# Inverse roots of all norms: from logarithm and exponential on ScalarE to a square root on ScalarE and a reciprocal on VectorE

## The chip, the cores and the metric

The kernel runs on one core of one Trainium2 chip, as one program. The metric is the device time of one execution in microseconds (us). Three runs of the kernel before took 2928.62, 2932.60 and 2936.35 us; their median, 2932.6 us, is the number to compare with.

## The reference, cut to what matters

Two blocks of two layers each work on 512 tokens of 1024 features (the second block has 256 context tokens beside them, so its first layer works on 768). Every layer is: norm, input projection, mixer, output projection, norm, gated feed-forward with a short convolution. What the change touches is the inverse root in all the norms:

```python
def rmsnorm(x, g):                       # first block; rmsnorm_2 of the second is the same
    xf = x.astype(jnp.float32)
    y = xf * lax.rsqrt(jnp.mean(xf * xf, axis=-1, keepdims=True) + EPS)
    return (y * g.astype(jnp.float32)).astype(x.dtype)

# token_mixer of the first block: each head's output is normed, gained and gated
ht = ht * lax.rsqrt(jnp.mean(ht * ht, axis=-1, keepdims=True) + EPS)
m_out = ht.reshape(B, S, MLSTM_W) * mh_norm_g * jax.nn.sigmoid(mo)

# retention_output of the second block: a group norm over each head's 64 values
mu = jnp.mean(y, axis=-1, keepdims=True)
var = jnp.mean((y - mu) ** 2, axis=-1, keepdims=True)
yn = ((y - mu) * lax.rsqrt(var + EPS)).reshape(B, L, RET_DIM) * gn_g
return silu(gate) * yn

# a layer of the first block
h = rmsnorm(x, g_pre_mix);  y = token_mixer(h, ...);  x = x + rmsnorm(y, g_post_mix)
h = rmsnorm(x, g_pre_ffn);  y = conv_ffn(h, ...);     x = x + rmsnorm(y, g_post_ffn)
```

## The kernel before

Features lie on the 128 partitions, tokens in the free dimension. A weight matrix comes as tiles of 128 output features; TensorE multiplies in float32r, and each product is made of three matmuls (high part by high part, high by low, low by high), `pe_chunk`, line 1011. So every weight tile and every activation is split in two: the high part by ScalarE (`split_high`, line 850, writes WH), the low part by VectorE (`split_low`, line 856, writes WL). Weight tiles go through a ring of 4 or 6 buffers.

A `Run` is a list of parts, each a head (the norm that makes the activations HH and HL of a part) and its segments (the projections). Each engine has its own program, written out in order: `scalar`, `vector`, `tensor`, `gpsimd` and `sync` of `Run`. The order of work on an engine is the order of that text; semaphores (`Signal`) tie the engines together.

The places with an inverse root:

- `Rstd` (lines 371 to 388) turns a mean of squares in PSUM bank pair PS[2] into RSTD, 128 partitions by 512 or 768 tokens. `act` does a logarithm (line 380) and an exponential with scale -0.5 (line 382) on ScalarE, and `wait` is what VectorE calls before it first reads RSTD. There are 13: four "late" ones in `GainHead` (512 tokens; the projection is computed from the unnormed rows and its result is multiplied by RSTD, line 970 into U or line 2211 into Z), four "first" ones (512 tokens; three in `GainHead`, one in `NormHead`: they scale Y, line 597, which is added to X, line 660 or 719), four in `NormHead` before line 727 (768 tokens in three, 512 in one), and one in `FinalHead` before line 767 (512), whose eight results are stored.
- `MixHead` (line 445): the same on MEAN2, 128x512, once in each layer of the first block. TensorE waits for it before the fourth chunk of the first three tiles (`begin`, line 484).
- `RetentionHead` (lines 507 to 588): three of 768 tokens in the first layer of the second block and three of 512 in the second. TensorE makes the three variances between the first and the second tile (line 579); ScalarE does the three logarithms (line 522), splits a weight tile, and does the three exponentials (line 527). VectorE splits that weight tile's low part (line 551), then does for each of the three rows a gain (line 555) and a gating (line 559), and then the low parts of activation chunks 5, 6 and 7 (line 537). TensorE goes through chunks 0 to 4 of tiles 1 and 2 meanwhile, and then needs chunk 5.

After the mean of squares TensorE does not stand still at once: `tensor` (line 1051) queues 24 small dummy matmuls (`idle`, line 257, 48 instructions) in which no result is used, and only then waits for the first chunk of HL (line 647 in `GainHead`, line 738 in `NormHead`). From that chunk on it takes three tiles chunk by chunk.

ScalarE evaluates its functions from a table set; `preload_act_table_set` loads a set ahead of its use, and where a function isn't in the loaded set a load stands right before it (an ACT_TABLE_LOAD with the function's line).

Of the kernel before, what the change touches and what calls it, by code (L numbers as in the profile page):

```python
# [10 lines left out]
ACT = mybir.ActivationFunctionType  # L11
AX = mybir.AxisListType

P = 128
D = 1024
# [98 lines left out]
def build(nc, a, out):  # L114
    ctx = ExitStack()
    with ctx:
# [129 lines left out]
        ysq_done, ysq_added = S("ysq_done"), S("ysq_added")  # L246
        log_done, rstd_done = S("log_done"), S("rstd_done")
        xsq_done, xsq_summed = S("xsq_done"), S("xsq_summed")
# [122 lines left out]
        class Rstd:  # L371
# [6 lines left out]
            def act(self, act):  # L378
                n = self.tokens
                act.activation(RSTD[:, 0:n], PS[2][:, 0:n], ACT.Ln, bias=EPSC[:, 0:1]).then_inc(log_done.sem, 1)  # L380
                act.wait_ge(log_done.sem, log_done.at(self.n + 1))
                act.activation(RSTD[:, 0:n], RSTD[:, 0:n], ACT.Exp, scale=-0.5).then_inc(rstd_done.sem, 1)  # L382

            def wait_log(self, eng):
                eng.wait_ge(log_done.sem, log_done.at(self.n + 1))

            def wait(self, eng):
                eng.wait_ge(rstd_done.sem, rstd_done.at(self.n + 1))

# [34 lines left out]
        class MixHead(Head):  # L424
# [20 lines left out]
            def act(self, act):  # L445
                act.activation(MEAN2, MEAN2, ACT.Ln, scale=float(D // P)).then_inc(head_ln.sem, 1)
                self.copied(act, 3)
                act.wait_ge(head_ln.sem, head_ln.at(1))
                act.activation(MEAN2, MEAN2, ACT.Exp, scale=-0.5).then_inc(head_rstd.sem, 1)
                for h in range(4):  # L450
                    act.wait_ge(head_out.sem, head_out.at(h + 1))
                    self.copied(act, 4 + h)
                for u in range(3, self.run.ring):
                    self.run.split_high(act, u)

            def dve(self, dve):
# [36 lines left out]
        class RetentionHead(Head):  # L493
# [13 lines left out]
            def act(self, act):  # L507
                n = self.tokens
                act.activation(Z[:, RG:RG + 3, 0:n], Z[:, RG:RG + 3, 0:n], ACT.Silu).then_inc(gate_done.sem, 1)  # L509
                act.preload_act_table_set("natural_log")  # L510
                self.copied(act, 0)
                self.copied(act, 1)
                self.run.split_high(act, 0)
                for c in range(3):
                    act.wait_ge(centred.sem, centred.at(c + 1))
                    act.activation(GROUP[c][:, 0:n], Z[:, RQ + c, 0:n], ACT.Square).then_inc(group_sq.sem, 1)
                for c in range(2, 5):
                    self.copied(act, c)
# [12 lines left out]
                for u in range(3, self.run.ring):  # L531
                    self.run.split_high(act, u)
# [7 lines left out]
            def dve(self, dve):  # L540
# [25 lines left out]
            def begin(self, pe, seg):  # L566
# [7 lines left out]
                for i, tile in enumerate(first):  # L574
                    if i == 1:
                        for c in range(3):
# [4 lines left out]
                            ins.then_inc(var_ps.sem, 1)  # L581
                        pe.wait_ge(group_ln.sem, group_ln.at(3))
                    for k in range(5):
# [8 lines left out]
        ROWS2 = [PO, PO + 1, NV, NV + 1, NV + 2, RG, RG + 1, RG + 2]  # L592
        mean_ps, centred, group_sq, var_ps, group_ln, group_rstd, group_out, gate_done = (
            S(n) for n in ("mean_ps", "centred", "group_sq", "var_ps", "group_ln", "group_rstd", "group_out", "gate_done"))

# [4 lines left out]
        class GainHead(Head):  # L600
# [72 lines left out]
        class NormHead(Head):  # L673
# [16 lines left out]
            def act(self, act):  # L690
                n = self.tokens
                self.before.wait_mean(act)
                if self.gain:
                    self.first.act(act)
                    act.preload_act_table_set("natural_log")
                    act.wait_ge(ctx_in.sem, ctx_in.at(16))
# [46 lines left out]
            def pe(self, pe):  # L743
                if self.gain:
                    self.first.wait_log(pe)
                    for c in range(DC):
# [29 lines left out]
        class Run:  # L776
# [149 lines left out]
            def act_out(self, act, tile):  # L926
# [25 lines left out]
                else:  # L952
                    if seg.squares and t == 0:
                        act.preload_act_table_set("natural_log")
                    if seg.out_act:
# [157 lines left out]
        def stream(run, mixer=None):  # L1113
# [35 lines left out]
            if parts[0][0].ready:  # L1149
                done(head_ln=1, head_rstd=1, head_ps=4, hg_done=4, head_out=4)  # L1150
            elif parts[0][0].begins:
                done(mean_ps=3, centred=3, group_sq=3, var_ps=3, group_ln=3, group_rstd=3, group_out=6, gate_done=1)
            done(**{f"w_loaded{s}": 16 * len(range(s, n, ring)) for s in range(ring)}, w_hi=n, w_lo=n, unit_done=n,
                 acc_free=tiles, own_done=run.n_hid, tap_done=run.n_hid, filtered=run.n_late,
                 silu_done=run.n_hid // 2, gated=run.n_hid // 2, g_hi=run.n_hid // 2, g_lo=run.n_hid // 2,
                 sq_done=run.n_sq, sq_added=run.n_added, sq_summed=run.n_summed,
                 ysq_done=run.n_ysq, ysq_added=run.n_ysum, log_done=run.n_rstd,
                 rstd_done=run.n_rstd, xsq_done=run.n_x, xsq_summed=run.n_x, t_done=run.n_t, h_hi=run.n_h,
# [3 lines left out]
        def region(offset, size):  # L1162
# [29 lines left out]
        qk_own, conv_done, qk_done = S("qk_own"), S("conv_done"), S("qk_done")  # L1192
        head_ln, head_rstd, head_ps, hg_done, head_out = (
            S(n) for n in ("head_ln", "head_rstd", "head_ps", "hg_done", "head_out"))
        ROWS1 = [AQ1, AQ1 + 1, AQ1 + 2, AQ1 + 3, V1, V1 + 1, V1 + 2, V1 + 3]
# [3 lines left out]
        class MixPrep:  # L1199
# [11 lines left out]
            def pe(self, pe, run, tile):  # L1211
                if tile.t == 7:
                    tile.seg.head.late.wait_log(pe)
                    pe.wait_ge(acc_free.sem, acc_free.at(tile.n - 6))
# [68 lines left out]
        def mix1(VEC, ahead):  # L1283
# [43 lines left out]
            with block() as b:  # L1327
# [131 lines left out]
                def _(act):  # L1459
# [45 lines left out]
                    for s in steps:  # L1505
# [21 lines left out]
                        if a + 1 == U - 1:  # L1527
                            act.preload_act_table_set("natural_log")

# [991 lines left out]
```

## Time and profile before

| | us |
|---|---|
| median of three runs | 2932.6 (2928.62 to 2936.35) |
| the profiled execution, its own time | 2934.65 |
| its span, first to last instruction | 2932.9 |
| TensorE busy in the span | 2856.3 (97%) |
| VectorE busy | 1763.2 (60%) |
| ScalarE busy | 1160.9 (40%) |
| GpSimd busy | 150.0 (5%) |

Every time below comes from the one profiled execution. L12 is line 12 of the kernel's text, PE is TensorE, DVE is VectorE, ACT is ScalarE. The granted TensorE clock was 0.995 of full speed over the span. In the timelines a row gives the start in us from the span's beginning, the duration of one instruction or of several that follow each other (x2 and so on), engine, line, operation, what it writes and reads, and in brackets how long the engine had stood idle before it and what ended that.

### The profile page before, as it was taken

Reading aid. Unit: us, or ns where it says so; the run is one execution under the profiler, and the core shown is the slowest. Engines: PE = TensorE matmul, PEld = TensorE weight load, DVE = VectorE, ACT = ScalarE, POOL = GpSimd, SP = SyncE. Lnnn points to the kernel's source line nnn. Section 1 sums busy time; section 2 is a strip of 40 time slices with the busy share of each in tenths; the row PEclk is TensorE's granted clock in tenths of the full one; section 3 lists DMA queues with packets and bytes.
Section 4 is the critical chain, followed back from the end, with each engine's and each line's share of the span. In section 5 each row is a group of like instructions: output and inputs, shape, how many; then the busy total and the mean of one; then the engine's idle time right before and its main releaser. Section 6 shows DMA issues by size and latency. Waiting matters only on the chain. (4 is left out here: it accounts for less than half of the span.)

```text
span 2932.9 us, 35827 instructions
## 1 busy us (share of the span) xinstructions
PE 2856.3 (97%) x14618; PEld 2408.2 (82%) x14618; DVE 1763.2 (60%) x2639; ACT 1160.9 (40%) x1709; POOL 150.0 (5%) x172
## 2 busy tenths in 40 slices
PE   9999999999999999999988999999999999999999
PEld 7657888878467888889965999999999975788887
DVE  6667866768567767667665565435534137564563
ACT  5255524443345424342255343213323236543342
POOL 0101000010110000000020100000000002100001
PEclk9999999999999999999999999999999999999999
DMA  5303243343112243326620111121122220232322
GB/s 204 108 15 108 93 134 105 93 130 122 44 59 86 90 147 100 116 85 232 212 66 30 58 58 65 57 73 65 58 58 65 65 97 23 101 101 84 111 83 83
DMA packets 84180, 269.95 MB, mean 92 GB/s; under 512 B 9264, under 2 KB 12208, under 8 KB 83632
## 3 DMA queue, kind: packets, MB, share of 16 engines
q1 hardware_dynamic: 84016, 267.66, 27.9%
q8 instruction: 116, 1.90, 0.3%
q14 instruction: 48, 0.39, 0.0%
HBM read 265.52 MB, written 2.10 MB: 91 GB/s over the span
## 5 line engine op out<-in xcount | busy, mean ns | idle before, releaser
L1011 PE MATMUL PS<-HH,WH 128*128 128x512 f32 (+1 forms) x3032 | 997.9, 366 | 23.7 <-DVE WL L856 8.1
L1011 PE MATMUL PS<-HH,WL 128*128 128x512 f32 (+1 forms) x3032 | 992.9, 364 | 0.0
L1011 PE MATMUL PS<-HL,WH 128*128 128x512 f32 (+1 forms) x3032 | 992.5, 364 | 0.0
L856 DVE TENSOR_TENSOR WL<-STAGE,WH 128x1024 fp32r<-128x1024 f32 (+2 forms) x420 | 482.7, 1151 | 497.5 <-ACT WH L850 497.2
L850 ACT ACTIVATE WH<-STAGE 128x1024 fp32r<-128x1024 f32 (+2 forms) x420 | 407.3, 973 | 621.5 <-DMA STAGE<-in_w_down 274.0
L1011 PEld LDWEIGHTS PS<-HH,WH 128*128 128x128 f32 x3032 | 559.5, 188 | 95.1 <-issue 11.9
L1011 PEld LDWEIGHTS PS<-HL,WH 128*128 128x128 f32 x3032 | 559.9, 188 | 65.4 <-issue 1.9
L1011 PEld LDWEIGHTS PS<-HH,WL 128*128 128x128 f32 x3032 | 559.7, 188 | 64.7
L1011 PE MATMUL PS<-GH,WL 128*128 128x512 f32 (+1 forms) x880 | 294.7, 367 | 0.0
L1011 PE MATMUL PS<-GL,WH 128*128 128x512 f32 (+1 forms) x880 | 294.7, 367 | 0.0
L1011 PE MATMUL PS<-GH,WH 128*128 128x512 f32 (+1 forms) x880 | 294.6, 367 | 0.0
L1011 PEld LDWEIGHTS PS<-GL,WH 128*128 128x128 f32 x880 | 162.7, 188 | 20.6
L1011 PEld LDWEIGHTS PS<-GH,WL 128*128 128x128 f32 x880 | 162.6, 188 | 20.6
L1011 PEld LDWEIGHTS PS<-GH,WH 128*128 128x128 f32 x880 | 162.6, 188 | 20.5
L984 DVE SCALAR_TENSOR_TENSOR CV<-PS,VEC,CV 128x384 f32<-128x384 f32 (+2 forms) x176 | 88.6, 546 | 95.9 <-ACT CV L942 94.4
L951 ACT ACTIVATE GH<-CV 128x512 fp32r<-128x512 f32 (+1 forms) x88 | 60.4, 686 | 190.6 <-DVE CV L993 190.6
L274 DVE SCALAR_TENSOR_TENSOR PS<-MODBUF,X 128x1024 f32<-128x1024 f32 x96 | 126.3, 1315 | 4.4
L984 DVE SCALAR_TENSOR_TENSOR CG<-PS,VEC,CG 128x384 f32<-128x384 f32 (+2 forms) x176 | 88.6, 546 | 56.4 <-ACT CG L942 54.8
L274 DVE SCALAR_TENSOR_TENSOR PS<-MODBUF,COND 128x1024 f32<-128x1024 f32 x64 | 78.9, 1233 | 56.2 <-DMA MODBUF<-in_w_mod 40.6
L970 DVE TENSOR_TENSOR U<-PS,RSTD 128x512 f32<-128x512 f32 x88 | 60.7, 690 | 85.2 <-PE PS L1011 73.7
L995 DVE TENSOR_TENSOR GL<-CV,GH 128x512 fp32r<-128x512 f32 (+1 forms) x88 | 66.8, 759 | 66.2 <-ACT GH L951 66.2
L325 POOL TENSOR_TENSOR SQSUM<-SQ,SQ 128x512 f32<-128x512 f32 (+1 forms) x8 | 12.4, 1555 | 1702.8 <-ACT SQ L318 1702.8
(233 smaller groups left out, 2544.9 us busy)
## 6 DMA issues: line engine op xcount, KB each, us to landing
STAGE<-in_w_up SPq DMA_DIRECT2D x176, 512.0 KB, 3.3
MODBUF<-in_w_mod SPq DMA_DIRECT2D x96, 512.0 KB, 4.2
STAGE<-in_w_in SPq DMA_DIRECT2D x84, 512.0 KB, 3.4
STAGE<-in_w_down SPq DMA_DIRECT2D x64, 384.0 KB, 3.1
STAGE<-in_w_down SPq DMA_DIRECT2D x64, 320.0 KB, 2.9
STAGE<-in_w_out SPq DMA_DIRECT2D x32, 512.0 KB, 4.7
BM<-in_na_bias SPq DMA_DIRECT2D x24, 256.0 KB, 2.6
CR<-in_const_ret SPq DMA_DIRECT2D x2, 1152.0 KB, 5.2
```

Of the source, the lines that this page charges most:

```text
L274: dve.scalar_tensor_tensor(out=PS[2][:].rearrange("p (c j) -> p c j", c=DC), in0=MODBUF[2 * self.l + buf][:], scalar=1.0, in1=cond, op0=AL ...
L325: pool.tensor_tensor(SQSUM[:, 0:tokens], SQ[0][:, 0:tokens] if c == 1 else SQSUM[:, 0:tokens], SQ[c % 2][:, 0:tokens], ALU.add).then_inc(s ...
L850: act.activation(WH[unit.slot][:, 0:size], STAGE[unit.slot][:, 0:size], ACT.Copy).then_inc(w_hi.sem, 1)
L856: dve.tensor_tensor(WL[unit.slot][:, 0:size], STAGE[unit.slot][:, 0:size], WH[unit.slot][:, 0:size].bitcast(F32), ALU.subtract).then_inc(w ...
L951: act.activation(seg.gh[:, t // 2, 0:n], CV[:, 0:n], ACT.Copy).then_inc(g_hi.sem, 1)
L970: dve.tensor_tensor(U[s][:, 0:n], self.whole(tile), RSTD[:, 0:n], ALU.mult).then_inc(acc_free.sem, 1)
L984: ins = dve.scalar_tensor_tensor(out=buf[:, a0 + shift:a0 + shift + an], in0=src[:, a0:a0 + an] if seg.late else self.acc(tile, col, an), ...
L995: dve.tensor_tensor(seg.gl[:, t // 2, 0:n], CV[:, 0:n], seg.gh[:, t // 2, 0:n].bitcast(F32), ALU.subtract).then_inc(g_lo.sem, 1)
L1011: ins = pe.matmul(self.acc(tile, col, tn), w[:, c:c + P], r[:, k, t0:t0 + tn], start=(k == 0 and m == 0), stop=(k == seg.kc - 1 and m == 2))
```

## The change

`Rstd.act` does a square root in place of the logarithm, and the exponential goes. `Rstd.wait`, on VectorE, does a reciprocal in place of waiting only. The same in `MixHead` (the reciprocal is ahead of the low part of chunk 3) and in `RetentionHead` (one reciprocal ahead of each gain). In `RetentionHead` VectorE's split of the third weight tile moves from ahead of the first row to behind it. The preloads name the set of the square root, and two preloads behind the first root of a head go. Semaphores are renamed (`log_done` to `root_done` and the like).

```diff
@@ class Rstd
             def act(self, act):
                 n = self.tokens
-                act.activation(RSTD[:, 0:n], PS[2][:, 0:n], ACT.Ln, bias=EPSC[:, 0:1]).then_inc(log_done.sem, 1)
-                act.wait_ge(log_done.sem, log_done.at(self.n + 1))
-                act.activation(RSTD[:, 0:n], RSTD[:, 0:n], ACT.Exp, scale=-0.5).then_inc(rstd_done.sem, 1)
+                act.activation(RSTD[:, 0:n], PS[2][:, 0:n], ACT.Sqrt, bias=EPSC[:, 0:1]).then_inc(root_done.sem, 1)
...
             def wait(self, eng):
+                eng.wait_ge(root_done.sem, root_done.at(self.n + 1))
+                eng.reciprocal(RSTD[:, 0:self.tokens], RSTD[:, 0:self.tokens]).then_inc(rstd_done.sem, 1)
                 eng.wait_ge(rstd_done.sem, rstd_done.at(self.n + 1))
@@ class MixHead, act and dve
-                act.activation(MEAN2, MEAN2, ACT.Ln, scale=float(D // P)).then_inc(head_ln.sem, 1)
+                act.activation(MEAN2, MEAN2, ACT.Sqrt, scale=float(D // P)).then_inc(head_root.sem, 1)
                 self.copied(act, 3)
-                act.wait_ge(head_ln.sem, head_ln.at(1))
-                act.activation(MEAN2, MEAN2, ACT.Exp, scale=-0.5).then_inc(head_rstd.sem, 1)
...
+                dve.wait_ge(head_root.sem, head_root.at(1))
+                dve.reciprocal(MEAN2, MEAN2).then_inc(head_rstd.sem, 1)
                 self.low(dve, 3)
@@ class RetentionHead, act
-                act.preload_act_table_set("natural_log")
+                act.preload_act_table_set("sqrt_and_others")
...
                 for c in range(3):
                     act.wait_ge(var_ps.sem, var_ps.at(c + 1))
-                    act.activation(GROUP[c][:, 0:n], PS[VAR_PS[c]][:, 0:n], ACT.Ln,
-                                   bias=EPSC[:, 0:1]).then_inc(group_ln.sem, 1)
+                    act.activation(GROUP[c][:, 0:n], PS[VAR_PS[c]][:, 0:n], ACT.Sqrt,
+                                   bias=EPSC[:, 0:1]).then_inc(group_root.sem, 1)
                 self.run.split_high(act, 2)
-                for c in range(3):
-                    act.wait_ge(group_ln.sem, group_ln.at(c + 1))
-                    act.activation(GROUP[c][:, 0:n], GROUP[c][:, 0:n], ACT.Exp, scale=-0.5).then_inc(group_rstd.sem, 1)
@@ class RetentionHead, dve
                 self.run.split_low(dve, 1)
-                self.run.split_low(dve, 2)
                 dve.wait_ge(gate_done.sem, gate_done.at(1))
                 for c in range(3):
+                    dve.wait_ge(group_root.sem, group_root.at(c + 1))
+                    dve.reciprocal(GROUP[c][:, 0:n], GROUP[c][:, 0:n]).then_inc(group_rstd.sem, 1)
                     dve.wait_ge(group_rstd.sem, group_rstd.at(c + 1))
...
+                    if c == 0:
+                        self.run.split_low(dve, 2)
@@ GainHead.act and NormHead.act, behind self.first.act(act)
-                    act.preload_act_table_set("natural_log")
@@ GainHead.act without gain, Run.act_out at the first tile with squares, mix1
-                    act.preload_act_table_set("natural_log")
+                    act.preload_act_table_set("sqrt_and_others")
```

## Rows read from the trace of the kernel before

**Rows 1.** The page's first section: busy time, share of the span, instructions.
```profile
PE 2856.3 (97%) x14618; PEld 2408.2 (82%) x14618; DVE 1763.2 (60%) x2639; ACT 1160.9 (40%) x1709; POOL 150.0 (5%) x172
```
**Rows 2.** Groups by line, ScalarE: busy us, mean ns, idle before.
```profile
L382 ACT ACT_TABLE_LOAD x13 | 16.7, 1283 | 0.2
```
**Rows 3.** Groups by line and shape, VectorE; one line's durations, min/median/max ns.
```profile
L993 DVE TENSOR_TENSOR CV<-CV,CG 128x768 f32<-128x768 f32 x22 | 21.1, 959 | 2.3
L1727 DVE TENSOR_TENSOR PP<-PP,CS 128x8 f32<-128x8 f32 x12 | 1.3, 160 | 0.0
...
L1587 DVE RECIPROCAL SM<-SM x32: 146/158/167, 138.5 to 831.7; 128x2 f32<-128x2 f32 x32
...
L274 DVE DVE_READ_ACCUMULATOR PS<-MODBUF,X 128x1 f32 x96 | 13.5, 140 | 0.0
```
**Rows 4.** Timeline around 259 us, first root of a GainHead.
```profile
259.19 0.69 ACT L380 ACTIVATE RSTD<-PS,EPSC 128x512 f32<-128x512 f32 x1 [0.27 <-PE PS L334]
...
258.95 1.23 DVE L856 TENSOR_TENSOR WL<-STAGE,WH 128x1024 fp32r<-128x1024 f32 x1 [1.64 <-ACT WH L850]
261.86 1.41 DVE L597 SCALAR_TENSOR_TENSOR Y<-Y,VEC,RSTD 128x512 f32<-128x512 f32 x2 [1.68 <-ACT RSTD L382]
```
**Rows 5.** Timeline around 629 us, VectorE.
```profile
628.46 2.36 DVE L856 TENSOR_TENSOR WL<-STAGE,WH 128x1024 fp32r<-128x1024 f32 x2 [1.64 <-ACT WH L850]
631.93 1.41 DVE L597 SCALAR_TENSOR_TENSOR Y<-Y,VEC,RSTD 128x512 f32<-128x512 f32 x2 [1.10 <-ACT RSTD L382]
```
**Rows 6.** Timeline around 1277 us, root of a NormHead, 768 tokens.
```profile
1277.25 0.90 ACT L380 ACTIVATE RSTD<-PS,EPSC 128x768 f32<-128x768 f32 x1 [1.68 <-PE PS L749]
...
1280.34 2.21 DVE L727 SCALAR_TENSOR_TENSOR T<-X,A,RSTD 128x512 f32<-128x512 f32 x4 [6.58 <-ACT RSTD L382]
```
**Rows 7.** Timeline around 2236 us, VectorE, 768 tokens.
```profile
2235.96 2.36 DVE L856 TENSOR_TENSOR WL<-STAGE,WH 128x1024 fp32r<-128x1024 f32 x2 [1.86 <-ACT WH L850]
2239.85 2.20 DVE L727 SCALAR_TENSOR_TENSOR T<-X,A,RSTD 128x512 f32<-128x512 f32 x4 [1.53 <-ACT RSTD L382]
```
**Rows 8.** Waits of TensorE: total us, times, longest.
```profile
PE PS L1011 <- DVE HL L647: 5.1, 5, 1.9
PE PS L1011 <- DVE HL L738: 4.1, 3, 1.4
```
**Rows 9.** Timeline around 917 us: a late root, VectorE and TensorE.
```profile
916.27 0.69 DVE L970 TENSOR_TENSOR U<-PS,RSTD 128x512 f32<-128x512 f32 x1 [5.54 <-ACT RSTD L382]
917.22 1.23 DVE L856 TENSOR_TENSOR WL<-STAGE,WH 128x1024 fp32r<-128x1024 f32 x1 [0.25 <-ACT WH L850]
...
918.59 0.47 PE L1011 MATMUL PS<-HH,WH 128*128 128x512 f32 x1 [2.29 <-DVE WL L856]
```
**Rows 10.** Timeline 1605 to 1620 us, RetentionHead, 768 tokens.
```profile
1605.89 0.90 ACT L522 ACTIVATE SQ<-PS,EPSC 128x768 f32<-128x768 f32 x1 [3.35 <-PE PS L579]
...
1612.60 1.02 DVE L555 SCALAR_TENSOR_TENSOR Z<-Z,VEC,SQ 128x768 f32<-128x768 f32 x1 [1.02 <-ACT SQ L527]
1618.37 2.69 DVE L537 TENSOR_TENSOR HL<-Z,HH 128x768 fp32r<-128x768 f32 x3
...
1619.93 0.51 PE L1011 MATMUL PS<-HH,WH 128*128 128x384 f32 x2
```
**Rows 11.** Timeline 2508 to 2519 us, RetentionHead, 512 tokens.
```profile
2508.46 0.69 ACT L522 ACTIVATE SQ<-PS,EPSC 128x512 f32<-128x512 f32 x1 [3.50 <-PE PS L579]
...
2513.88 0.75 DVE L555 SCALAR_TENSOR_TENSOR Z<-Z,VEC,SQ 128x512 f32<-128x512 f32 x1 [0.81 <-ACT SQ L527]
...
2518.05 1.89 DVE L537 TENSOR_TENSOR HL<-Z,HH 128x512 fp32r<-128x512 f32 x3
...
2518.79 0.50 PE L1011 MATMUL PS<-HH,WH 128*128 128x512 f32 x1 [0.79 <-DVE HL L537]
```
**Rows 12.** Timeline 2922 to 2933 us, the final norm.
```profile
2922.21 0.69 ACT L380 ACTIVATE RSTD<-PS,EPSC 128x512 f32<-128x512 f32 x1 [1.22 <-PE PS L334]
...
2924.87 5.39 DVE L767 SCALAR_TENSOR_TENSOR X<-X,FIN,RSTD 128x512 f32<-128x512 f32 x8 [4.54 <-ACT RSTD L382]
```

More of the change, by code:

```diff
@@ L246, in build @@
         ysq_done, ysq_added = S("ysq_done"), S("ysq_added")
-        log_done, rstd_done = S("log_done"), S("rstd_done")
+        root_done, rstd_done = S("root_done"), S("rstd_done")
         xsq_done, xsq_summed = S("xsq_done"), S("xsq_summed")
@@ L379, in act, with wait_root @@
                 n = self.tokens
-                act.activation(RSTD[:, 0:n], PS[2][:, 0:n], ACT.Ln, bias=EPSC[:, 0:1]).then_inc(log_done.sem, 1)
-                act.wait_ge(log_done.sem, log_done.at(self.n + 1))
-                act.activation(RSTD[:, 0:n], RSTD[:, 0:n], ACT.Exp, scale=-0.5).then_inc(rstd_done.sem, 1)
-            def wait_log(self, eng):
-                eng.wait_ge(log_done.sem, log_done.at(self.n + 1))
+                act.activation(RSTD[:, 0:n], PS[2][:, 0:n], ACT.Sqrt, bias=EPSC[:, 0:1]).then_inc(root_done.sem, 1)
+            def wait_root(self, eng):
+                eng.wait_ge(root_done.sem, root_done.at(self.n + 1))
             def wait(self, eng):
+                eng.wait_ge(root_done.sem, root_done.at(self.n + 1))
+                eng.reciprocal(RSTD[:, 0:self.tokens], RSTD[:, 0:self.tokens]).then_inc(rstd_done.sem, 1)
                 eng.wait_ge(rstd_done.sem, rstd_done.at(self.n + 1))
@@ L581, in begin @@
                             ins.then_inc(var_ps.sem, 1)
-                        pe.wait_ge(group_ln.sem, group_ln.at(3))
+                        pe.wait_ge(group_root.sem, group_root.at(3))
                     for k in range(5):
@@ L592, in build @@
         ROWS2 = [PO, PO + 1, NV, NV + 1, NV + 2, RG, RG + 1, RG + 2]
-        mean_ps, centred, group_sq, var_ps, group_ln, group_rstd, group_out, gate_done = (
-            S(n) for n in ("mean_ps", "centred", "group_sq", "var_ps", "group_ln", "group_rstd", "group_out", "gate_done"))
+        mean_ps, centred, group_sq, var_ps, group_root, group_rstd, group_out, gate_done = (
+            S(n) for n in ("mean_ps", "centred", "group_sq", "var_ps", "group_root", "group_rstd", "group_out", "gate_done"))
         def scale_y(dve, gain, c):
@@ L694, in act @@
                     self.first.act(act)
-                    act.preload_act_table_set("natural_log")
                     act.wait_ge(ctx_in.sem, ctx_in.at(16))
@@ L744, in pe @@
                 if self.gain:
-                    self.first.wait_log(pe)
+                    self.first.wait_root(pe)
                     for c in range(DC):
@@ L953, in act_out @@
                     if seg.squares and t == 0:
-                        act.preload_act_table_set("natural_log")
+                        act.preload_act_table_set("sqrt_and_others")
                     if seg.out_act:
@@ L1149, in stream @@
             if parts[0][0].ready:
-                done(head_ln=1, head_rstd=1, head_ps=4, hg_done=4, head_out=4)
+                done(head_root=1, head_rstd=1, head_ps=4, hg_done=4, head_out=4)
             elif parts[0][0].begins:
-                done(mean_ps=3, centred=3, group_sq=3, var_ps=3, group_ln=3, group_rstd=3, group_out=6, gate_done=1)
+                done(mean_ps=3, centred=3, group_sq=3, var_ps=3, group_root=3, group_rstd=3, group_out=6, gate_done=1)
             done(**{f"w_loaded{s}": 16 * len(range(s, n, ring)) for s in range(ring)}, w_hi=n, w_lo=n, unit_done=n,
@@ L1156, in stream @@
                  sq_done=run.n_sq, sq_added=run.n_added, sq_summed=run.n_summed,
-                 ysq_done=run.n_ysq, ysq_added=run.n_ysum, log_done=run.n_rstd,
+                 ysq_done=run.n_ysq, ysq_added=run.n_ysum, root_done=run.n_rstd,
                  rstd_done=run.n_rstd, xsq_done=run.n_x, xsq_summed=run.n_x, t_done=run.n_t, h_hi=run.n_h,
@@ L1192, in build @@
         qk_own, conv_done, qk_done = S("qk_own"), S("conv_done"), S("qk_done")
-        head_ln, head_rstd, head_ps, hg_done, head_out = (
-            S(n) for n in ("head_ln", "head_rstd", "head_ps", "hg_done", "head_out"))
+        head_root, head_rstd, head_ps, hg_done, head_out = (
+            S(n) for n in ("head_root", "head_rstd", "head_ps", "hg_done", "head_out"))
         ROWS1 = [AQ1, AQ1 + 1, AQ1 + 2, AQ1 + 3, V1, V1 + 1, V1 + 2, V1 + 3]
@@ L1212, in pe @@
                 if tile.t == 7:
-                    tile.seg.head.late.wait_log(pe)
+                    tile.seg.head.late.wait_root(pe)
                     pe.wait_ge(acc_free.sem, acc_free.at(tile.n - 6))
@@ L1527, in _ @@
                         if a + 1 == U - 1:
-                            act.preload_act_table_set("natural_log")
+                            act.preload_act_table_set("sqrt_and_others")
                 @b.gpsimd
```

## The prediction

> **What bounds the kernel now.** I read the page's busy line first: TensorE is busy for 97% of the span [rows 1], so only work that makes TensorE wait, or that stands behind its last matmul, can move the time. Next I looked at its waits by who ended them, and at the timeline around every inverse root. A root is one of the few places where TensorE runs dry: the mean of squares ends, dummy matmuls fill some microseconds, and then it waits for the first low part of the new activations. The waits for these are 5.1 and 4.1 us in total [rows 8]: the dummies leave only 1 to 2 us open at each place. So a shorter chain gains at most that, for the dummies stay; a longer chain has no such limit, every microsecond of it is lost. Behind the first chunk TensorE is the slower of the two, so nothing more is lost or won there.
>
> **The change part by part.** *What goes.* Thirteen times a logarithm is followed by a table load of 1.28 us [rows 2] and an exponential, before VectorE goes on. At the final norm these three take from 2922.21 to 2924.87, 2.66 us [rows 12], of which the root's own 0.69 stays. So 1.97 us go at 512 tokens. At 768 the chain is 1277.25 to 1280.34, 3.09 us, of which 0.90 stays [rows 6], and 2.19 go. ScalarE's time as such is worth nothing, it is 40% busy [rows 1]; so is what the dropped preloads free.
>
> *What comes.* A reciprocal of 128x512 or 128x768 on VectorE, in the same chain. The trace has none of that size. It has 128x2: 146/158/167 ns [rows 3]. A sum of two tensors takes 160 ns at 8 elements and 959 at 768, so 1.05 ns an element over a fixed 152 ns [rows 3]. Lower bound: a reciprocal streams as a sum does, 152 + 512 x 1.05 = 0.69 us and 0.96 us at 768. The small reciprocals give the element's price only loosely: (158 - 152)/2 = 3 ns by the median, (167 - 152)/2 = 7.5 ns by the longest, and with the fixed part no larger than an accumulator read's 140 ns [rows 3] it would be 9 ns. I take 4 ns, near the median, a little above since the spread is upward: 152 + 512 x 4 = 2.20 us, and 3.22 us at 768. The upper bound is 9 ns, 4.8 and 7.1 us.
>
> The Trainium skill ("VectorE: DVE Perf Modes", First, the fixed hardware budget) says that a reciprocal is an iterated divide with a repeat count of 8; what eight passes would give is a rival below.
>
> *Where VectorE is when the root is there.* It is not always idle, as the exponential's chain ran beside its weight splits. I put 0.03 us between dependent instructions, as the rows have it.
> - Three places like [rows 4]: the root ends at 259.19 + 0.69 = 259.88, VectorE's split ends at 260.18. Reciprocal to 260.21 + 2.20, next step at 262.44 in place of 261.86: 0.58 us later. Two are heads of the first block, lost in full: 1.2. The third is the NormHead of 512 tokens, where TensorE has none of the three waits [rows 8], so some cover: 0.3.
> - Two like [rows 5], with two splits: free at 630.82, next step 633.08 in place of 631.93: 1.15 each, 2.3. One of them feeds the squares of the next norm, of which each is waited for in turn, so it is lost too.
> - Two like [rows 6]: root's end 1278.15, next step 1281.43 in place of 1280.34: 1.09 each, 2.2.
> - One like [rows 7], 768 tokens with two splits: free at 2238.32, next 2241.60 in place of 2239.85: 1.75.
> - The final norm [rows 12]: 2922.90 + 0.06 + 2.20 = 2925.16 in place of 2924.87: 0.3, lost in full, for the stores follow.
> - Four late roots, needed only when VectorE empties an accumulator. TensorE has three more accumulators by then, so three cost nothing; if that cover were gone they would cost the same 0.3 each. At the fourth TensorE waits 2.29 us for a weight's low part that stands on VectorE behind the root and one U [rows 9]. The chain there is as long as in the final norm: 0.3.
> - MixHead twice: TensorE has three chunks of three tiles to do before it needs MEAN2, and the chain grows by 0.3 only: 0. The low part of chunk 3 is now queued behind the reciprocal, but TensorE takes it after MEAN2 anyway.
>
> *RetentionHead, twice.* Here three reciprocals stand one after another, and chunk 5 waits for all of them, where before two exponentials ran beside VectorE's work. At 768 tokens [rows 10]: first root at 1605.89 + 0.90 = 1606.79, before VectorE is wanted elsewhere. From there three reciprocals 3 x 3.25 = 9.75, three pairs of gain and gating 1618.37 - 1612.60 = 5.77, the moved split 1.23 (a split's time in [rows 4]), one low part 2.69/3 = 0.90. Chunk 5 is there at 1624.47; TensorE took it at 1619.93, with 0.66 us to spare. Loss 4.5 us. At 512 tokens [rows 11]: 2509.15 + 0.03 + 3 x 2.23 + 4.17 + 1.23 + 0.63 = 2521.90, TensorE started at 2518.79 after a wait of 0.79: loss 3.1 us. The moved split itself is early enough: behind the first row, at about 1613, while TensorE needs that tile only after one whole tile of five chunks, begun when the three variances were taken. It would cost up to its 1.23 us if that were wrong, and it frees VectorE to start the first reciprocal, so the move is at worst neutral.
>
> Sum: 1.2 + 0.3 + 2.3 + 2.2 + 1.75 + 0.3 + 0.3 + 4.5 + 3.1 = 15.9 us slower. The profiled execution took 2934.65, so 2950.6; it stands 2.05 above the median of the runs, and against that median 2932.6 the forecast is 2949. Per ns of the element's price the sum moves by 0.512 at seven places, 0.768 at three, and three times as much in each RetentionHead: 3.6 + 2.3 + 2.3 + 1.5 = 9.7 us.
>
> The Trainium skill ("ScalarE: Activation LUTs", What ACT_TABLE_LOAD costs) gives a switch 1.28 us of load and 1.38 us of drain, 2.66 us in all. The load agrees with the trace; of the drain the trace shows nothing, since from the logarithm's start to VectorE's next step there are 2.66 us with both functions in it. By that rule twelve removed loads would give back 1.38 us more each; the sum goes by the rows.
>
> **The rivals.**
> - *A cheap reciprocal, the other sign.* At 1.05 ns an element every chain is shorter. Gains: 0.93 at the two first-block places like [rows 4], 0 at the third (TensorE does not wait there), 0.36 twice, 1.17 twice, 0.51, final norm 1.22, late root 1.22, RetentionHead 0 (TensorE did not wait) and 0.79 (all that it waited). Sum 8.7, so 2924. For it: a median of 158 ns, below what 8 elements of a sum cost. Against it: two elements weigh too little to tell, and the longest, 167. It decides below 4 - 15.9/9.7 = 2.4 ns an element, a reciprocal of 1.4 us.
> - *Eight passes for each element,* by the rule above: 8 x 1.05 = 8.4 ns, 4.45 us and 6.60 us. Then 5.7 + 2.6 + 6.8 + 8.9 + 5.1 + 2.5 + 2.5 + 14.7 + 9.9 = 58.7 us, so 2991. For it: the fixed part of a one-input instruction may be as small as 140 ns [rows 3], which with 16.8 for two elements gives 157, the median. Against it: with a fixed 152 ns it would be 169, above the longest of the 32.
> - *The load stays.* If the square root's set isn't there when the root comes, a load of 1.28 us stands ahead of each. On top of the forecast that is 1.28 at nine norms, the late root and at most once in each RetentionHead: about 14 us more, 2963. Against it: the preloads move along with the function.
>
> **How the numbers follow.** Forecast (2 to 6 ns) 0.45, eight passes 0.35, cheap 0.15, load stays 0.05. The likeliest case alone spans 2929 (2 ns) to 2968 (6 ns). The range takes in most of the eight passes and of the cheap side: 2928 to 2990. Less than 0.3% (8.8 us) can hardly be told from no change in this kernel. The sum passes 8.8 us at 3.3 ns. So faster by more 0.05 (the cheap case reaches only 8.7), within it 0.25 (rest of the cheap case, lower part of the forecast), slower 0.70.
>
> **What would show it.** RECIPROCAL rows of 128x512 near 2.2 us and 128x768 near 3.2 us on VectorE: this number decides. No table load between the root and the reciprocal. TensorE's waits for the first low part grow from 1 to 2 us by 0.6 to 1.8 each, and new waits of 3 to 5 us stand before chunk 5 in both RetentionHeads, where the first had none. The three other late roots and MixHead show no new wait of TensorE. I am wrong if the reciprocal is below 1.4 us (then not slower), or if these two waits are not there although it is 2 us or more.

## The result and the profile after

| | before | after |
|---|---|---|
| median (four runs each) | 2933.42 (2928.62 to 2936.35) | 2988.99 (2987.38 to 2991.7) |
| span of the profiled execution, us | 2932.9 | 2987.8 |
| granted TensorE clock, mean over the span | 0.995 | 0.985 |

The changed kernel takes 1.0193 times as long, 95% interval 1.0176 to 1.0209: 55.6 us slower. The forecast was 2949 with a range of 2928 to 2990. The sign is right, the size is 3.5 times what I had worked out, and the time lies at the very edge of the range.

The first section of the page after answers to [rows 1], and the groups of VectorE's reciprocals by line and shape to [rows 3] (busy us, mean ns | idle before):

```profile
PE 2878.1 (96%) x14618; PEld 2424.2 (81%) x14618; DVE 1841.6 (62%) x2660; ACT 1122.6 (38%) x1669; POOL 149.8 (5%) x172
...
L387 DVE RECIPROCAL RSTD<-RSTD 128x512 f32<-128x512 f32 x10 | 33.5, 3350 | 21.4 <-ACT RSTD L380 21.4
L387 DVE RECIPROCAL RSTD<-RSTD 128x768 f32<-128x768 f32 x3 | 14.9, 4951 | 7.8 <-ACT RSTD L380 7.8
...
L1585 DVE RECIPROCAL SM<-SM 128x2 f32<-128x2 f32 x32 | 5.1, 159 | 5.3 <-ACT PX L1477 5.3
```

The number that was to decide is 3350 ns at 512 elements and 4951 at 768: (4951 - 3350)/256 = 6.25 ns an element over a fixed 150 ns. No table load stands between root and reciprocal: VectorE's idle time before a reciprocal was ended by the root itself (ACT RSTD L380). The two elements of the last row would come to 150 + 12.5 = 162 ns; 159 is what they take, so the small shape fits the price and could not have told it.

Waits of TensorE after (total us, times, longest), to hold against [rows 8] and [rows 10, 11]:

```profile
PE PS L1009 <- DVE HL L534: 15.7, 3, 9.1
PE PS L1009 <- DVE HL L736: 14.4, 4, 4.8
...
PE PS L1009 <- DVE HL L646: 10.2, 4, 4.1
PE PS L1009 <- DVE WL L854: 8.4, 6, 3.4
...
PE PS L747 <- ACT SQ L699: 3.2, 1, 3.2
```

L646 and L736 are the lines 647 and 738 of before: 9.2 us have become 24.6. L534 is line 537 of before; its two long waits, 9.1 and 6.4 us, are those for chunk 5 in the RetentionHeads. Before, it was

```profile
PE PS L1011 <- DVE HL L537: 1.0, 2, 0.8
```

so 1.0 us have become 15.7. The last line is the mean that is summed chunk by chunk, which waited 1.0 us before. These waits are where the reciprocal's length shows. But they don't hold all of the loss, and the timeline around 630 us shows the rest. After, the place of [rows 5]:

```profile
630.12 2.36 DVE L854 TENSOR_TENSOR WL<-STAGE,WH 128x1024 fp32r<-128x1024 f32 x2 [1.64 <-ACT WH L848]
632.39 3.35 DVE L387 RECIPROCAL RSTD<-RSTD 128x512 f32<-128x512 f32 x1
635.77 1.42 DVE L597 SCALAR_TENSOR_TENSOR Y<-Y,VEC,RSTD 128x512 f32<-128x512 f32 x2
...
639.77 0.80 PE L1009 MATMUL PS<-HH,WH 128*128 128x512 f32 x1 [4.10 <-DVE HL L646]
640.37 0.63 PE L1009 MATMUL PS<-HL,WH 128*128 128x512 f32 x1
```

and before, the same matmuls:

```profile
635.93 0.50 PE L1011 MATMUL PS<-HH,WH 128*128 128x512 f32 x1 [1.91 <-DVE HL L647]
636.27 0.40 PE L1011 MATMUL PS<-HL,WH 128*128 128x512 f32 x1
```

VectorE is where the forecast's steps put it: splits, then at once the reciprocal, then the next step 0.03 us behind it. TensorE waits 4.10 us in place of 1.91, and then the same matmul takes 0.63 us in place of 0.40. The windows say why (columns: us, then busy us and instructions of PE, PEld, DVE, ACT, POOL, then the granted clock, the DMA's share, GB/s). Before, then after, the stretch around the first matmuls behind the norm:

```profile
634.00:641.00 7.00, 5.09 (x23) 4.19 (x23) 7.00 (x12) 5.26 (x8) 0.00 (x0) 1.00 0.01 2
```

```profile
638.00:645.00 7.00, 5.23 (x13) 4.14 (x14) 7.00 (x12) 5.22 (x9) 0.00 (x0) 0.51 0.01 2
```

In the same seven microseconds TensorE does 23 matmuls at a granted clock of 1.00 before, and 13 at 0.51 after: the lower of its two levels, 1.2 GHz in place of 2.4. The fall comes inside the wait: TensorE's last dummy ends at 635.7, and the clock is still at 1.00 two microseconds later and low from 638 on.

```profile
637.00:638.00 1.00, 0.00 (x0) 0.00 (x0) 1.00 (x3) 0.17 (x1) 0.00 (x0) 1.00 0.00 0
638.00:639.00 1.00, 0.00 (x0) 0.00 (x0) 1.00 (x3) 1.00 (x2) 0.00 (x0) 0.53 0.00 0
```

Over the whole span the clock stands at half speed for 90 us, where before it was 27. Most of this is not in the waits, where it would cost nothing. Counted over the stretches of half clock in the two traces, TensorE works during 68.8 of these us, and during 26.5 before. At full speed the same work takes half as long, so the 42 us more cost an estimated 21. They were in no term of my sum.

In the RetentionHead at 768 tokens, the place of [rows 10], the three reciprocals stand as forecast (the second and third behind a gain and a gating each), and the moved split behind the first row:

```profile
1627.26 0.90 ACT L522 ACTIVATE SQ<-PS,EPSC 128x768 f32<-128x768 f32 x1 [3.38 <-PE PS L579]
...
1628.27 4.95 DVE L551 RECIPROCAL SQ<-SQ 128x768 f32<-128x768 f32 x1 [2.94 <-ACT SQ L522]
...
1635.19 1.22 DVE L854 TENSOR_TENSOR WL<-STAGE,WH 128x1024 fp32r<-128x1024 f32 x1
1636.32 4.94 DVE L551 RECIPROCAL SQ<-SQ 128x768 f32<-128x768 f32 x1
1636.55 0.59 PE L1009 MATMUL PS<-HH,WH 128*128 128x384 f32 x2 [0.28 <-DVE WL L854]
...
1651.14 1.01 PE L1009 MATMUL PS<-HH,WH 128*128 128x384 f32 x2 [9.14 <-DVE HL L534]
```

The first pair of matmuls behind the 9.14 us takes 1.01 us, where it took 0.51 in [rows 10]. In three of the four norms that TensorE needs late, and in MixHead, nothing of this is seen: in MixHead, where MEAN2 lies in the tile XF, the reciprocal runs from 209.88 to 213.23 and TensorE takes MEAN2 at 215.61 without a wait. (The fourth late root, [rows 9], is another matter: see below.)

```profile
209.88 3.35 DVE L468 RECIPROCAL XF<-XF 128x512 f32<-128x512 f32 x1 [1.58 <-ACT XF L446]
...
215.61 1.88 PE L486 MATMUL PS<-XF,CST 128*128 128x512 f32 x4
```

### The profile page after: what moved, and what is told of

It reads as the page before. It is cut to its first block and busy times, and to the rows that moved or that the text cites. A ratio compares the mean times of both kernels' runs of the same rounds, so it can differ in the third digit from the quotient of the medians.

```text
span 2987.8 us, 35808 instructions
## 1 busy us (share of the span) xinstructions
PE 2878.1 (96%) x14618; PEld 2424.2 (81%) x14618; DVE 1841.6 (62%) x2660; ACT 1122.6 (38%) x1669; POOL 149.8 (5%) x172
## 5 line engine op out<-in xcount | busy, mean ns | idle before, releaser
L1009 PE MATMUL PS<-HH,WH 128*128 128x512 f32 (+1 forms) x3032 | 1004.4, 368 | 54.2 <-DVE HL L534 15.7
L1009 PEld LDWEIGHTS PS<-GH,WH 128*128 128x128 f32 x880 | 162.7, 188 | 20.6
L1009 PEld LDWEIGHTS PS<-GH,WL 128*128 128x128 f32 x880 | 162.7, 188 | 20.6
L1009 PEld LDWEIGHTS PS<-GL,WH 128*128 128x128 f32 x880 | 162.6, 188 | 20.6
```

Of the source, the lines that this page charges most:

```text
L1009: ins = pe.matmul(self.acc(tile, col, tn), w[:, c:c + P], r[:, k, t0:t0 + tn], start=(k == 0 and m == 0), stop=(k == seg.kc - 1 and m == 2))
```

## The experiments

The theory after the first look: the reciprocal costs 6.25 ns an element in place of 4, which by my own sum is 15.9 + 9.7 x 2.25 = 37.7 us; the remaining 18 us are TensorE at half clock behind the longer stalls. The rivals: the structure of the sum is wrong (waits that I left out), or the clock is a bystander and the reciprocal's chain alone costs 55 us. Lines of the diffs are cut to the core.

**e1_min: all large reciprocals become a cheap two-input operation.**

```diff
-                eng.reciprocal(RSTD[:, 0:self.tokens], RSTD[:, 0:self.tokens])
+                eng.scalar_tensor_tensor(out=RSTD[:, 0:self.tokens], in0=RSTD[:, 0:self.tokens], scalar=0.05,
+                                         in1=RSTD[:, 0:self.tokens], op0=ALU.min, op1=ALU.min)
```

> The changed kernel with every large reciprocal left out and a minimum with 0.05 of the same tile in its place (so the norms are not the reference's): same engine, same place, same waits, only the price per element differs. If the loss is the reciprocal's duration and nothing else of the change (square root, removed loads, moved split), this is my cheap case: instructions of 0.7 us and 1.0 us, and 2924 us, at most 2930. If part of the 55 us comes from the new order on VectorE or from the extra wait between the engines, it stays above 2935.

Measured: 2920.17 us (2919.44 to 2922.03), 0.9957 times before (0.9942 to 0.9971), clock 0.996. The operation takes the place of the reciprocal at 689 ns:

```profile
L387 DVE SCALAR_TENSOR_TENSOR RSTD<-RSTD 128x512 f32<-128x512 f32 x10 | 6.9, 689 | 17.6 <-ACT RSTD L380 17.6
```

So the whole loss of 55.6 us and 13 more hang on the duration of that one instruction. The rest of the change (the moves, the semaphores, the preloads), taken together, does not make the kernel slower. My cheap rival had said 2924 for this duration; 4 us less came out. Part of that is the clock: at [rows 9] TensorE worked for 3.4 us at half clock before, behind its wait of 2.29 us, and in this kernel, behind 0.73 us, it does not, which is about 1.6 us.

**e2_half: the reciprocal with the duration that I had forecast.** Half of the columns get a reciprocal, the other half the cheap operation.

```diff
-                eng.reciprocal(RSTD[:, 0:self.tokens], RSTD[:, 0:self.tokens])
+                eng.reciprocal(RSTD[:, 0:self.tokens // 2], RSTD[:, 0:self.tokens // 2])
+                eng.scalar_tensor_tensor(out=RSTD[:, self.tokens // 2:self.tokens], ..., op0=ALU.min, op1=ALU.min)
```

> The changed kernel with the reciprocal on the first half of the columns and the minimum with 0.05 on the other half (norms not the reference's): 1.75 + 0.40 us at 512 tokens and 2.55 + 0.55 at 768, which is what my forecast took for one reciprocal (2.20 and 3.22). If only the duration was mis-sized, this comes out at the forecast, 2947 to 2951 us. If stalls cost more than their length because TensorE's granted clock falls in them, it lies above by what half-clock time it shows in the records, 2952 to 2960.

Measured: 2949.66 us (2947.94 to 2951.87), 1.0055 (1.0038 to 1.0072), clock 0.993. Groups by shape:

```profile
L387 DVE RECIPROCAL RSTD<-RSTD 128x256 f32<-128x256 f32 x10 | 17.5, 1750 | 17.6 <-ACT RSTD L380 17.6
L387 DVE RECIPROCAL RSTD<-RSTD 128x384 f32<-128x384 f32 x3 | 7.7, 2551 | 4.8 <-ACT RSTD L380 4.8
...
L388 DVE SCALAR_TENSOR_TENSOR RSTD<-RSTD 128x256 f32<-128x256 f32 x10 | 3.6, 361 | 0.0
```

1.75 + 0.36 = 2.11 us stand where I had 2.20 (and about 3.04 where I had 3.22), and the time is the forecast's 2949 within a microsecond. That it comes so near is in part luck. With these shorter pairs my sum gives about 14 us, not 15.9; and the clock is in the result too, since TensorE works for 37.4 us at half clock here and for 26.5 before, an estimated 5 us more. The stalls of this kernel (at most 3.7 us) are shorter than those of the change and fewer of them meet the low clock, so e2 shows that the miss hangs on the duration, but not that the sum is complete. With 256 and 384 elements the price is also confirmed: 150 + 6.25 x 256 = 1750, 150 + 6.25 x 384 = 2550.

**e3_fill: the changed kernel with more dummy matmuls in the stalls.** The reciprocals and every chain stay as they are; TensorE is only kept busy longer where it would stand still.

```diff
-                idle(pe, 24, 3)
+                idle(pe, 24 + self.more(seg), 3)      # 4, 12, 16 or 19 more, by the norm that follows
@@ NormHead, behind the mean summed in chunks
-                    idle(pe, 24, 3)
+                    idle(pe, 40, 3)
@@ RetentionHead, ahead of chunk 5
+                    idle(pe, 36 if self.tokens == TOK else 25, 2)
```

> The changed kernel with more dummy matmuls in the stalls: 4 to 19 more calls after each mean of squares, 16 more behind the one summed chunk by chunk, 36 and 25 ahead of chunk 5 in the two RetentionHeads, each a little shorter than the wait it stands in. Theory one (the reciprocal costs 38 us by its length, and 17 us more because TensorE's granted clock falls to half after these stalls): the half-clock time falls from 85 us to about 30, and the time to 2968 to 2975 us. Rival (all of the loss is chain length, the low clock costs nothing): 2987 to 2991, or above, since dummies only take up TensorE.

Measured: 2969.97 us (2969.08 to 2970.54), 1.0125 (1.011 to 1.014), clock 0.995. 336 more dummy matmul instructions make the kernel 19.0 us faster, and the half-clock time in which TensorE works goes from 68.8 to 22.0 us. Its waits of TensorE, and below them the stretch ahead of chunk 5 of the RetentionHead, in which TensorE stood still for 9.14 us in the changed kernel:

```profile
PE PS L1010 <- DVE HL L737: 2.1, 4, 0.6
PE PS L1010 <- DVE HL L534: 2.1, 3, 1.1
...
PE PS L1010 <- DVE HL L647: 1.7, 4, 0.6
```

```profile
1632.00:1642.00 10.00, 8.91 (x76) 8.72 (x75) 9.93 (x7) 3.02 (x4) 0.00 (x0) 1.00 0.01 2
```

The stalls are as long as ever, for VectorE is busy for 9.93 of the 10 us, but they are filled, and the clock is at 1.00. What is left is 36.6 us over before: my sum at the true price, 37.7. This separates the two parts of the result: about 37 us for the reciprocal's length, 19 us for the clock.

The Trainium skill ("Perfetto Trace Analysis", Matmul Optimizations) says that the matmul engine scales its power with its utilization, so that matmuls should run back-to-back. By that rule dummies in the stalls should pay, and the traces agree: 19.0 us.

**e5_split_first: the moved split goes back.**

```diff
+                self.run.split_low(dve, 2)
...
                 for c in range(3):
...
-                    if c == 0:
-                        self.run.split_low(dve, 2)
```

> The changed kernel with the third weight tile's split on VectorE put back ahead of the first reciprocal in the two RetentionHeads. My forecast called the move at worst neutral. By the rows: the split must wait for ScalarE's high part, so VectorE would begin the first reciprocal 4.8 us (768 tokens) and 3.9 us (512) later and have 1.2 us less to do after it: chunk 5 comes 3.6 and 2.7 us later, 2995 us, or 2997 with half-clock time. Rival (the move does nothing): 2989.

Measured: 2996.22 us (2993.42 to 3000.09), 1.0216 (1.0201 to 1.0232), 7.2 us more than the change as it is. The timeline at the 768-token place:

```profile
1627.90 0.90 ACT L522 ACTIVATE SQ<-PS,EPSC 128x768 f32<-128x768 f32 x1 [4.40 <-PE PS L578]
...
1632.37 1.23 DVE L853 TENSOR_TENSOR WL<-STAGE,WH 128x1024 fp32r<-128x1024 f32 x1 [7.41 <-ACT WH L847]
1633.51 4.95 DVE L552 RECIPROCAL SQ<-SQ 128x768 f32<-128x768 f32 x1
...
1655.24 1.01 PE L1008 MATMUL PS<-HH,WH 128*128 128x384 f32 x2 [13.13 <-DVE HL L534]
```

The root is there at 1628.80, but VectorE stands 7.41 us idle for a high part that ScalarE only makes behind the roots; the reciprocal starts at 1633.51 in place of 1628.27 (0.64 of it because this trace is that much later here), and the wait for chunk 5 is 13.13 us in place of 9.14. The time came out as expected. The move is a part of the change that earns something, and I had called it no more than harmless.

**e6_heads_before: only the 13 norms of Rstd are changed,** MixHead and RetentionHead are as before.

```diff
-                    dve.reciprocal(GROUP[c][:, 0:n], GROUP[c][:, 0:n]).then_inc(group_rstd.sem, 1)
...
+                for c in range(3):
+                    act.wait_ge(group_ln.sem, group_ln.at(c + 1))
+                    act.activation(GROUP[c][:, 0:n], GROUP[c][:, 0:n], ACT.Exp, scale=-0.5).then_inc(group_rstd.sem, 1)
```

> Only the change to Rstd (thirteen roots); MixHead and RetentionHead keep logarithm and exponential. If the parts add up, this leaves out what the two RetentionHeads lose between the variances and chunk 5 (11.3 and 9.1 us between the two traces) and nothing for MixHead: 2969 us. If the parts interact (a stall of one changes what the next costs) it is off by more than 4 us.

Measured: 2967.09 us (2965.77 to 2970.64), 1.012 (1.0103 to 1.0137), clock 0.990. Of the 55.6 us, 33.7 belong to Rstd and 21.9 to the two heads. Its waits for the first low parts are those of the full change:

```profile
PE PS L1009 <- DVE HL L736: 14.4, 4, 4.8
...
PE PS L1009 <- DVE HL L646: 10.4, 4, 4.1
```

The parts don't interact by more than the error (2969 was expected). In the trace of the full change the first matmul behind the stall has slipped by 9.8 us against before at the 768-token RetentionHead and by 6.7 at the other; when the clock is back at 1.00 it is 11.8 (the expectation has 11.3) and 9.1, 20.9 together. So MixHead's share is about 1 us at most, within the error.

**e8_no_dummies: the kernel before, without the 24 dummies behind each mean.** If stalls alone bring the clock down, it must show without any reciprocal.

```diff
-                    idle(pe, 24, 3)
@@ Run.tensor
-                            idle(pe, 24, 3)
```

> The kernel before, without the dummy matmuls behind the means of squares (no other edit, no chain longer): TensorE stands still for 6 to 8 us there in place of 1 to 2. If a stall costs its length and then half-clock time, each of the eight places adds some 3.4 to 6.8 us at half clock, which costs half of that: 2947 to 2961 us. Rival (low clock after a stall costs nothing measurable): 2934.

Measured: 2954.34 us (2953.49 to 2955.53), 1.0073 (1.0058 to 1.0088), clock 0.983. Its waits, then the first matmul behind the first such place, then the window around it:

```profile
PE PS L1010 <- DVE HL L738: 25.2, 4, 6.8
PE PS L1010 <- DVE HL L647: 21.0, 4, 7.3
```

```profile
267.10 0.79 PE L1010 MATMUL PS<-HH,WH 128*128 128x512 f32 x1 [6.70 <-DVE HL L647]
```

```profile
262.00:273.00 11.00, 5.90 (x15) 4.69 (x16) 9.90 (x16) 8.42 (x13) 0.00 (x0) 0.53 0.00 0
```

With the wait at L749 (6.4 us in place of 1.0), the waits grew by 42.4 us, where the dummies had filled 8 x 5.5 = 44 us (the ninth place, at the final norm, has nothing of TensorE behind it). So no chain is longer; TensorE only stands still where it did work of no use. Yet the kernel is 20.6 us slower. TensorE works for 65.7 us at half clock in place of 26.5, and half of these 39 us more is 20: this is the clock alone, in a kernel with the old roots. With e3 it is shown from both sides.

**e4_one_set and e10_one_set: the kernel before, but with the set preloaded that has both functions.** VectorE gets no reciprocal, and the 13 loads between logarithm and exponential go.

```diff
-                act.preload_act_table_set("natural_log")
+                act.preload_act_table_set("natural_log_exp_and_others")
```

(The two preloads that the change drops are dropped too.)

> The kernel before (logarithm and exponential on ScalarE) with the preloads naming the set natural_log_exp_and_others, which holds both, and without the two preloads behind the first root. If the table load between the two was a real part of the chain, the chain is 1.28 us shorter at each root, capped by what TensorE waits: about 1.3 at eight places, 1.2 at two more, 0.8 in the second RetentionHead, together about 12 us: 2921 us. Rival (dummies and splits hide it): 2933.

> The one-set kernel (logarithm and exponential from natural_log_exp_and_others) again, to compare with the two kernels of this call on one chip: 2915 to 2919 us; the one-function kernel 0 to 4 us below it.

Measured: 2916.76 us (2912.62 to 2919.19), 0.9943 (0.9928 to 0.9957), and again, beside e9, 2918.51 (2918.35 to 2920.69), 0.9947 (0.9935 to 0.996). Timeline of the first norm:

```profile
261.69 0.69 ACT L380 ACTIVATE RSTD<-PS,EPSC 128x512 f32<-128x512 f32 x1 [0.27 <-PE PS L334]
262.41 0.63 ACT L382 ACTIVATE RSTD<-RSTD 128x512 f32<-128x512 f32 x1
```

The exponential follows the logarithm 0.03 us later, in the place of a load of 1.28 [rows 2]. The gain is 17.5 and 15.7 us against the kernel before on the same chip, with waits for the first low parts down to 1.1 and 0.2 us, the clock at 0.996. The expectation was 12. The clock accounts for an estimated 4 to 5 us of the gain: TensorE works for 18.3 and 15.7 us at half clock in these two, and for 26.5 before. Apart from the clock, this is about all that the change could have won at these places, since the dummies stay and end no earlier.

**e7_one_op: one function for the whole root,** Abs_reciprocal_sqrt in place of the logarithm and the exponential, with its set preloaded.

```diff
-                act.activation(RSTD[:, 0:n], PS[2][:, 0:n], ACT.Ln, bias=EPSC[:, 0:1]).then_inc(log_done.sem, 1)
-                act.wait_ge(log_done.sem, log_done.at(self.n + 1))
-                act.activation(RSTD[:, 0:n], RSTD[:, 0:n], ACT.Exp, scale=-0.5).then_inc(rstd_done.sem, 1)
+                act.activation(RSTD[:, 0:n], PS[2][:, 0:n], ACT.Abs_reciprocal_sqrt, bias=EPSC[:, 0:1]).then_inc(rstd_done.sem, 1)
```

> The kernel before with one ScalarE function (Abs_reciprocal_sqrt) in place of logarithm and exponential everywhere, its set preloaded, nothing on VectorE. The chain is 0.63 us (512) or 0.85 us (768) shorter again than with both functions in one set. If what TensorE still waits behind the dummies there (0.2 us at six places, 0.9 where two splits stand on VectorE) is all that is left, only the final norm and the late root gain 0.6 each: 2914 to 2916 us. If the chain were still open at the other places, it would be some 5 us more, 2910.

Measured: 2918.71 us (2912.6 to 2921.35), 0.9945 (0.9932 to 0.9959). The expectation missed: a chain 0.66 us shorter than in e4 gives nothing measurable (e10, beside it, took 2918.51, so the 0 to 4 us below it that e10 expected of this kernel are not there either). The timeline, which begins at 260.76 in the middle of the 48 dummies, shows the first low part ready at 264.57 and the first matmul at 264.81, straight behind the last dummies:

```profile
260.76 4.29 PE L257 MATMUL PS<-MEAN 128*128 128x128 f32 x37
...
263.83 0.74 DVE L640 SCALAR_TENSOR_TENSOR HL<-X,VEC,HH 128x512 fp32r<-128x512 f32 x1
...
264.81 0.48 PE L1003 MATMUL PS<-HH,WH 128*128 128x512 f32 x1
```

Here the dummies are what TensorE runs on when the data are there.

**e9_one_op_fewer: the same with fewer dummies.**

```diff
-                            idle(pe, 24, 3)
+                            idle(pe, 15 if short else 21, 3)      # short: ahead of the 512-token NormHead
```

> The same with 21 dummy calls in place of 24 behind the means, and 15 ahead of the norm of 512 tokens. If the dummies are now what TensorE runs on when the first low part is there, each place gives back up to 0.6 us (0.69 us of dummies), the last one some 1.5: 2910 to 2912 us. If the clock needs them as they are, half-clock stretches come back and it is 2915 or above.

Measured: 2911.8 us (2909.25 to 2913.29), 0.9922 (0.9909 to 0.9936), clock 0.998. Waits:

```profile
PE PS L1003 <- DVE HL L640: 2.4, 4, 1.4
...
PE PS L1003 <- DVE HL L730: 0.5, 1, 0.5
```

This is the best version of the study, some 22 us below before and 77 us below the change. That it lies 7 us below e7 is not shown to be the dummies' work. In the two profiles the difference is 8.8 us, and TensorE works for 23.0 us at half clock in e7 and for 9.6 in e9, an estimated 6.7 us; the stretches that differ (around 768, 1484, 1590 and 2409 us) are none of those where dummies went. Only the place with 15 dummies shows a gain of its own above 1 us, 1.8 us.

## Why the prediction was wrong in size, point by point

**What held.** TensorE is the bound, and a root matters only where TensorE runs dry behind it: no new wait came up elsewhere. The chains run as worked out (splits, reciprocal, next step 0.03 us behind). No load stands between root and reciprocal. The three late roots and MixHead cost nothing to be seen. In both RetentionHeads chunk 5 became late. And the places and slopes of the sum hold: put together with 3.35 and 4.95 us they give 37.7 us, and by the two traces the first matmul behind each wait (at the final norm the end of the program) slipped by 37.3 us in all.

**The step that failed** is "I take 4 ns" for an element. It is 6.25, and by my own slope that is 22 us of the 40 that were missing. I had chosen by the row of 128x2, in which two elements stand over a fixed part of 150 ns: between 4 and 6.25 ns there are 4.5 ns in 159, and the row's spread is 21. The true price lies outside my likeliest case (2 to 6 ns) and below the eight passes, between the two. The estimate should have been held as open between 1.05 and 9 and not put "near the median"; the middle of these bounds, 5 ns, would have been nearer. The Trainium skill ("VectorE: DVE Perf Modes", First, the fixed hardware budget) names a repeat count of 8 for the divide, from which I had 8.4 ns. The measurement decides against this too: 6.25 ns are six times the 1.05 of a sum.

**The step that was missing** is TensorE's clock. I wrote that every microsecond by which the chain grows is lost, and took it as one microsecond. The slips of the same matmul between the two traces, taken from ahead of the wait to where the clock is back at 1.00, say otherwise. Worked out with 3.35 and 4.95 us, [rows 5] would have lost 2.3 and lost 4.5; the one at 1674 (as [rows 6]) 2.8 and lost 5.5; [rows 7] 3.5 and lost 5.5; the late root of [rows 9] 1.4 and lost 2.4; the RetentionHeads 9.7 and 6.6, and lost 11.8 and 9.1. At each of them the first matmul alone slipped by what was worked out, within 0.4 us; the rest came in the microseconds behind it, at half clock. Over all places that rest is 19.1 us, less 1.5 where the kernel before had a half-clock stretch (at 2503) that the change has not. Where the clock stayed up, the formula is right: at [rows 4] 1.7 was worked out and 1.6 lost, and the matmul behind the stall takes 0.50 us as before:

```profile
267.53 0.50 PE L1009 MATMUL PS<-HH,WH 128*128 128x512 f32 x1 [2.96 <-DVE HL L646]
```

At 886, a place of the same kind, 1.7 was worked out and 3.1 lost, and behind a wait as long the first matmul takes 0.79:

```profile
901.09 0.79 PE L1009 MATMUL PS<-HH,WH 128*128 128x512 f32 x1 [2.97 <-DVE HL L646]
```

So the length of the wait alone does not decide it. At the final norm of [rows 12], with no matmul behind it, 1.4 was worked out and 1.5 lost. At 1266 the chunked mean itself was caught: it waited 3.20 us in place of 1.00, and its 32 matmuls take 13.59 us in place of 10.56.

```profile
1280.46 13.59 PE L747 MATMUL PS<-SQ,MEAN 128*128 128x512 f32 x32 [3.20 <-ACT SQ L699]
```

```profile
1266.65 10.56 PE L749 MATMUL PS<-SQ,MEAN 128*128 128x512 f32 x32 [1.00 <-ACT SQ L701]
```

The dummies in the kernel before were the hint that I had read and not used. They fill 5.5 us at each place, and a stretch that they no longer reach has a price of its own. e3 puts it at 19 us in this kernel, e8 at 20.6 for the stalls of 6 to 7 us that open in the kernel before without them.

**"At worst neutral"** of the moved split held, but hid a gain. With a slow reciprocal VectorE's start decides, and the move saves 7.2 us. "Early enough" was slightly wrong: TensorE waits 0.28 and 0.78 us for it, but both are swallowed by the wait for chunk 5, which VectorE sets.

**The rivals.** *Eight passes* named the time (2991) for a wrong reason: 8.4 ns without the clock give about the same as 6.25 with it, which is chance. Had the clock been in the sum, eight passes would have come out above 3000. So a total that fits doesn't confirm its mechanism; the duration in the trace does. *A cheap reciprocal* would have been the faster side, and e1 has it at 2920.

*The load stays* is out: no table load has the root's line in the trace after.

**What stays open.** Why two waits of 2.96 and 2.97 us differ in what the clock does behind them. No run removes one stall alone, so what each costs by the clock is known from the slips only. Of the 4 us by which e1 lies below my cheap case 1.6 are found; whether the two dropped preloads have a share isn't shown. And how much of e9's gain over e7 is the dummies'.

## What to carry to other kernels

Price an operation at the size at which it will run: a row of two elements is nearly all fixed cost (150 of 159 ns), and a chain on which TensorE waits multiplies the error by every place. Before a function is split over two engines to get rid of a table load, look for one set that has both functions: the same 13 loads went for a faster kernel here (0.994) and for a slower one (1.019). And where a change makes TensorE stand still for more than it did, count the stall twice, once for its length and once for the matmuls behind it at half clock, or fill it.

## What the runs showed of the hardware

- A reciprocal on VectorE, float32 on 128 partitions, takes 150 ns and 6.25 ns an element (159 ns at 2, 1750 at 256, 2551 at 384, 3350 at 512, 4951 at 768). The price of an element is six times that of a two-input sum (1.05 ns).
- Behind waits of 4.1 and 9.1 us the granted clock was 0.51 and 0.50; a matmul took 0.63 us in place of 0.40, and a pair 1.01 in place of 0.51. Behind a wait of 1.91 us it was 1.00. Behind one of 2.96 us the first matmul took 0.50, behind one of 2.97 us 0.79. 24 dummies at each of nine places are worth 20.6 us, and 4 to 36 more in the longer stalls 19.0.
- Abs_reciprocal_sqrt is one activation for the whole inverse root, with its set preloaded as cheap as a square root (686 ns against 683 at 128x512), and it is in the fastest kernel of the study (2911.8 us).
